# The test for over 128 tokens moved behind the first stores, and the last sums and the last store cut in halves

## The reference, cut to what matters

```python
def moe_swiglu(h, w_router, w_gate, w_up, w_down):
    ...
    for e in range(N_EXPERTS):
        ye = swiglu(t, w_gate[e], w_up[e], w_down[e]).astype(jnp.float32)
        out = out + gates[:, e:e + 1] * ye
...
        x = x + rms_norm(f_out, post_ffn_gain[l])
    return x
```

## Time and profile before

| | |
|---|---|
| median of 3 runs | 1172.28 us (1172.23 to 1173.7) |
| the profiled execution's own time | 1173.94 us |
| its span in the trace | 1172.2 us |
| PE busy | 1111.1 us (95%) |
| DVE busy | 889.5 us (76%) |
| ACT busy | 750.3 us (64%) |
| stores of the output | 2 of 512 KB |

### The profile page before, as it was taken

The page is one execution under the profiler, slowest core; times in us unless marked ns, Lnnn a source line. Parts: engine busy times, 40 slices in busy tenths (PEclk is TensorE's granted clock), DMA queues, the critical chain, the costliest instruction groups (busy, mean ns, idle before and its releaser), DMA issues.

```text
span 1172.2 us, 13852 instructions
## 1 busy us (share of the span) xinstructions
PE 1111.1 (95%) x5410; PEld 927.7 (79%) x5410; DVE 889.5 (76%) x743; ACT 750.3 (64%) x738; POOL 40.1 (3%) x76
## 2 busy tenths in 40 slices
PE   5998999997996699999999999999999999999995
PEld 5986888885994588888888888888888888888783
DVE  5666545456276489888888989888898988888895
ACT  5555433445365177777777777777767777777764
POOL 3000000000001000000000000000000000001100
PEclk9999999998998699999999999999999999999998
DMA  8647655551424499999999999999999999999981
GB/s 264 239 155 249 201 193 179 179 179 58 149 93 165 175 344 375 388 377 383 383 377 394 373 372 396 371 385 384 371 387 382 374 388 383 379 370 373 397 305 74
DMA packets 174594, 350.65 MB, mean 299 GB/s; under 512 B 9248, under 2 KB 58416, under 8 KB 174528
## 3 DMA queue, kind: packets, MB, share of 16 engines
q1 hardware_dynamic: 169792, 332.96, 78.0%
q0 software_dynamic: 4592, 16.30, 4.1%
q10 hardware_dynamic: 144, 0.52, 0.2%
HBM read 343.97 MB, written 5.77 MB: 298 GB/s over the span
## 4 chain that ended last, share of the span: by engine, by line
PE 88%; DVE 6%; ACT 3%; issue 2%; DMA 1%; DVEq 0%; SPq 0%; ACTq 0%
PE ps L1140 28%; PE ps L1141 27%; PE ps L1142 27%; PE ps L1417 2%; DVE lo_gu L1899 1%; PE ps L1147 1%; DMA raw_gu<-in_w_in 1%; PE ps L1460 1%; PE ps L1218 1%; DVE lo_d L1906 1%; DVE rows L1647 0%; DMA raw_d<-in_moe_w_down 0%; DVE xt_lo L1629 0%; PE ps L1199 0%; PE ps L1334 0%
## 5 line engine op out<-in xcount | busy, mean ns | idle before, releaser
L1899 DVE TENSOR_TENSOR lo_gu<-raw_gu,hi_gu 128x2048 fp32r<-128x2048 f32 x176 | 396.2, 2290 | 64.7 <-ACT hi_gu L992 64.7
L1140 PE MATMUL ps<-hi_gu,xt_hi 128*128 128x512 f32 (+1 forms) x1040 | 405.1, 390 | 9.1 <-DVE xt_lo L1629 4.3
L1142 PE MATMUL ps<-hi_gu,xt_lo 128*128 128x512 f32 (+1 forms) x1040 | 398.7, 383 | 0.0
L1141 PE MATMUL ps<-lo_gu,xt_hi 128*128 128x512 f32 (+1 forms) x1040 | 398.1, 383 | 0.0
L992 ACT CAST hi_gu<-raw_gu 128x2048 fp32r<-128x2048 f32 x176 | 327.9, 1910 | 11.2 <-PE ps L1142 8.1
L1002 ACT CAST hi_d<-raw_d 128x1024 fp32r<-128x1024 f32 x172 | 172.2, 1050 | 132.8 <-PE ps L1142 132.8
L1140 PEld LDWEIGHTS ps<-hi_gu,xt_hi 128*128 128x128 f32 x1040 | 198.3, 191 | 47.9 <-DVE xt_lo L1629 5.5
L1142 PEld LDWEIGHTS ps<-hi_gu,xt_lo 128*128 128x128 f32 x1040 | 198.2, 191 | 38.2
L1141 PEld LDWEIGHTS ps<-lo_gu,xt_hi 128*128 128x128 f32 x1040 | 198.4, 191 | 35.3
L1906 DVE TENSOR_TENSOR lo_d<-raw_d,hi_d 128x1024 fp32r<-128x1024 f32 x172 | 202.8, 1220 | 18.3 <-ACT hi_d L1002 17.6
L1140 PE MATMUL ps<-hi_d,ht_hi 128*128 128x512 f32 x424 | 167.9, 396 | 0.3 <-DVE ht_lo L1913 0.3
(11 more groups left out here) (241 smaller groups left out, 784.4 us busy)
## 6 DMA issues: line engine op xcount, KB each, us to landing
raw_gu<-in_moe_w_gate SPq DMA_DIRECT2D x176, 512.0 KB, 5.8
raw_gu<-in_moe_w_up SPq DMA_DIRECT2D x176, 512.0 KB, 7.2
raw_d<-in_moe_w_down SPq DMA_DIRECT2D x88, 1024.0 KB, 7.9
raw_gu<-in_dense_w_gate SPq DMA_DIRECT2D x22, 512.0 KB, 3.7
raw_gu<-in_dense_w_up SPq DMA_DIRECT2D x22, 512.0 KB, 4.7
raw_d<-in_dense_w_down SPq DMA_DIRECT2D x11, 1024.0 KB, 4.8
raw_gu<-in_w_in SPq DMA_DIRECT2D x16, 512.0 KB, 8.7
raw_gu<-in_w_out SPq DMA_DIRECT2D x16, 512.0 KB, 6.8
```

What stands on the lines that cost most here:

```text
L1140: pe.matmul(o, a_hi, b_hi, start=first, stop=False)
L1141: pe.matmul(o, a_hi, b_lo, start=False, stop=False)
L1142: return pe.matmul(o, a_lo, b_hi, start=False, stop=last)
L1899: dve.tensor_tensor(flat_piece(lo_gu, slot_at), flat_piece(raw_gu, slot_at), flat_piece(hi_gu, slot_at).bitcast(F32), ALU.subtract).then_i ...
```

## The change

- The test for a second round (read, test, jump) goes from ahead of the last sums to the very end of each of DVE, ACT and SP. PE's stays where it is.
- The last sums go by column halves: four of 128x512, in the order in which PE's four scatters end, each with its own semaphore step, where before there were two of 128x1024.
- The new `finish` does the gain, the reciprocal and the residual sum of one tile; tile 0 is finished ahead of tile 1's gain multiply. The result goes to `acc`, no longer to `x_res`. Tile 1's residual sum is cut into two column halves.
- SP stores tile 0 and the left half of tile 1; the right half is stored by ACT's queue.
- If there is a second round, it starts from `rows`, takes a norm of its own (two more columns in `sum_sq`, `root`, `rstd`) and stores both tiles once more. It doesn't run with these inputs.

```diff
@@ SP
+            sp.wait_ge(x_updated, FINAL + 1)
+            sp.dma_start(out[0, 0:P, :], acc[:, 0, :]).then_inc(out_stored, 16)
+            sp.wait_ge(x_updated, FINAL + 2)
+            sp.dma_start(out[0, P:2 * P, 0:512], acc[:, 1, 0:512]).then_inc(out_stored, 16)
             sp.wait_ge(slots_ready, 1)
             count = sp.value_load(overflow[0:1, 0:1], min_val=0, max_val=S)
             with sp.If(count > P):
...
-            for t in range(TT):
-                sp.wait_ge(x_updated, TT * (2 * DEPTH - 1) + t + 1)
-                sp.dma_start(out[0, t * P:(t + 1) * P, :], x_res[:, t, :]).then_inc(out_stored, 16)
-            sp.wait_ge(out_stored, 16 * TT)
+            sp.wait_ge(out_stored, 16 * (TT + 1))
@@ ACT
             experts()
+            for t in range(TT):
+                act.wait_ge(summed, TT + t + 1)
+                norm(norm_id(1, POST_FFN, t), rows[:, t, :], y_sb[:], D)
+            act.wait_ge(x_updated, FINAL + TT + 1)
+            act.dma_start(out[0, P:2 * P, 512:D], acc[:, 1, 512:D]).then_inc(out_stored, 16)
             act.wait_ge(slots_ready, 1)
             count = act.value_load(overflow[0:1, 0:1], min_val=0, max_val=S)
             with act.If(count > P):
                 overflow_experts()
-            for t in range(TT):
-                act.wait_ge(summed, t + 1)
-                norm(norm_id(1, POST_FFN, t), rows[:, t, :], y_sb[:], D)
@@ PE
-                        last = pe.matmul(o, picks, half_of(xt_lo, 0)[:, ks, :], start=False, stop=True)
-                        if n == 1:
-                            last.then_inc(last_scattered, 1)
+                        pe.matmul(o, picks, half_of(xt_lo, 0)[:, ks, :], start=False, stop=True
+                                  ).then_inc(last_scattered, 1)
@@ DVE
+            def finish(idx, total, to, pieces):
+
+                s, fill = gain_of(1, POST_FFN)
+                t = idx % TT
+                dve.wait_ge(gain_loaded[s], gain_level(s, fill))
+                dve.tensor_tensor(to[:, t, :], total[:, t, :], gains[s][:], ALU.mult).then_inc(gained, 1)
+                r = scale_of(idx)
+                dve.wait_ge(gained, idx - norm_id(1, POST_FFN, 0) + 1)
+                for n in range(pieces):
+                    cols = slice(n * D // pieces, (n + 1) * D // pieces)
+                    dve.scalar_tensor_tensor(to[:, t, cols], to[:, t, cols], r, x_res[:, t, cols], ALU.mult, ALU.add
+                                             ).then_inc(x_updated, 1)
...
             experts()
+            for n in range(2):
+                cols = slice(n * 512, (n + 1) * 512)
+                for t in range(TT):
+                    dve.wait_ge(last_scattered, n * TT + t + 1)
+                    dve.scalar_tensor_tensor(rows[:, t, cols], ps[:, B_GU + 2 * t + n, :], last_gate[:, t:t + 1],
+                                             acc[:, t, cols], ALU.mult, ALU.add).then_inc(summed, 1)
+            dve.wait_ge(summed, 2 * TT)
+            for t in range(TT):
+                finish(norm_id(1, POST_FFN, t), rows, acc, t + 1)
             count = dve.value_load(overflow[0:1, 0:1], min_val=0, max_val=S)
             with dve.If(count > P):
                 overflow_experts()
-            s, fill = gain_of(1, POST_FFN)
-            dve.wait_ge(gain_loaded[s], gain_level(s, fill))
-            for t in range(TT):
-                add_last(t, rows).then_inc(summed, 1)
-                dve.wait_ge(summed, t + 1)
-                dve.tensor_tensor(acc[:, t, :], rows[:, t, :], gains[s][:], ALU.mult).then_inc(gained, 1)
-            for t in range(TT):
-                r = scale_of(norm_id(1, POST_FFN, t))
-                dve.wait_ge(gained, t + 1)
-                dve.scalar_tensor_tensor(x_res[:, t, :], acc[:, t, :], r, x_res[:, t, :], ALU.mult, ALU.add
-                                         ).then_inc(x_updated, 1)
```

More of the change, by code:

```diff
@@ L166, in build_trunk @@
         eps = sb("eps", [P, 1])
-        sum_sq = sb("sum_sq", [P, 12 * TT])
-        root = sb("root", [P, 12 * TT])
-        rstd = sb("rstd", [P, 12 * TT])
+        sum_sq = sb("sum_sq", [P, 13 * TT])
+        root = sb("root", [P, 13 * TT])
+        rstd = sb("rstd", [P, 13 * TT])
         sinks = sb("sinks", [P, DEPTH, N_HEADS])
@@ L397, in build_trunk @@
         out_stored = sem("out_stored")
+        FINAL = TT * (2 * DEPTH - 1)
         gain_plan = []
@@ L604, in _ @@
             with sp.If(count > P):
-                sp.wait_ge(early_summed, TT)
+                sp.wait_ge(last_added, TT)
                 for t in range(TT):
@@ L613, in _ @@
                         load_expert(i, q, e, None)
-            for t in range(TT):
-                sp.wait_ge(x_updated, TT * (2 * DEPTH - 1) + t + 1)
-                sp.dma_start(out[0, t * P:(t + 1) * P, :], x_res[:, t, :]).then_inc(out_stored, 16)
-            sp.wait_ge(out_stored, 16 * TT)
+                for t in range(TT):
+                    sp.wait_ge(x_updated, FINAL + TT + 1 + t + 1)
+                    sp.dma_start(out[0, t * P:(t + 1) * P, :], rows[:, t, :]).then_inc(out_stored, 16)
+                sp.wait_ge(out_stored, 16 * (2 * TT + 1))
+            sp.wait_ge(out_stored, 16 * (TT + 1))
         @block.gpsimd
@@ L1096, in overflow_experts @@
             def overflow_experts():
+                act.wait_ge(last_lo_done, 2)
+                act.copy(spare[:, 2:3], eps[:, 0:1]).then_inc(y_copied, 1)
                 with act.Fori(0, E // 2) as i:
@@ L1114, in overflow_experts @@
                         act.copy(y_sb[:], banks(B_Y, 2)).then_inc(y_copied, 1)
+                act.wait_ge(expert_added, TT * E)
+                for t in range(TT):
+                    norm(6 * DEPTH * TT + t, acc[:, t, :], y_sb[:], D)
             act.wait_ge(const_made, 4)
@@ L1990, in experts @@
                 dve.wait_ge(last_gate_ready, 1)
[L1992 to L1995, removed]
+            def finish(idx, total, to, pieces):
[9 more added lines that the diff above has]
+                                             ).then_inc(x_updated, 1)
             def overflow_experts():
+                dve.wait_ge(out_stored, 16 * (TT + 1))
                 for t in range(TT):
-                    add_last(t, acc).then_inc(last_added, 1)
+                    dve.tensor_copy(acc[:, t, :], rows[:, t, :]).then_inc(last_added, 1)
                 dve.wait_ge(last_added, TT)
-                dve.memset(last_gate[:], 0.0).then_inc(last_gate_ready, 1)
                 with dve.Fori(0, E // 2) as i:
@@ L2025, in overflow_experts @@
                 dve.wait_ge(expert_added, TT * E)
-                dve.wait_ge(last_gate_ready, 2)
+                for t in range(TT):
+                    finish(6 * DEPTH * TT + t, acc, rows, 1)
             dve.wait_ge(const_made, 4)
```

## The result

The changed kernel takes 1177.27 us, median of 22 runs (1174.85 to 1178.09); the kernel before, run beside it, takes 1175.11 us, median of 22 (1170.68 to 1176.63). The ratio is 1.0022, with a 95% interval of 1.0015 to 1.003: slower by 0.22%, 2.2 to 2.6 us. I had forecast 1170.2 us, 2.1 us faster, in a range of 1168.9 to 1172.1. The direction was wrong, and so was the range.

What follows compares the result with a forecast made beforehand. TensorE bounds the whole span, but VectorE's late sums bound the end; VectorE gains 3.06 us, about 1 us is given back to ScalarE's final jump, so 1172.28 − 2.1 = 1170.2 us, range 1168.9 to 1172.1.

Steps and rivals of the forecast that it cites:

- none of that is touched: Everything before the last 15 us, TensorE's chain with its weight loads: claimed unaffected, so no cost was counted there.
- a second fetch at the end: Rival at the final jumps: instructions up to the barrier need two fetches; time 1174.8 us, chance 0.06.
- rival 1: At the end, ScalarE's jump is hidden and the stores end the span; time 1168.9 us, chance 0.13.
- rival 2: At the end, ScalarE's instruction fetch slips by 1.9 us behind data packets; time 1171.0 to 1172.1 us, chance 0.17.
- The jump leaves the head: VectorE behind the last xt_lo: the first half sum starts at 1157.98 instead of 1161.34, 3.36 us earlier.
- Half sums: VectorE's last sums: four halves, 0.67 us from start to start, the last ending at 1160.74.
- Two finishes: VectorE's gain, reciprocal and residual steps for both tiles: ends at 1166.06 instead of 1169.12, 3.06 us earlier.
- ScalarE: Squares and roots at the end: both 1.28 us table loads go, roots ready before the reciprocals, price nothing.
- The jumps arrive at the end: Final jumps: ScalarE's branch ends at 1167.3, its 2.5 us jump finishes last at 1169.8, span ends 1170.1.
- The stores: Last output stores: a half lands in 2.0 to 2.7 us, by 1168.1 to 1168.8, before ScalarE's jump is through.
- From span to time: Conversion to kernel time: the span's 2.1 us gain was taken whole off the unprofiled median.
- The base: Starting time of the forecast: median 1172.28 us without a profile, from three runs spanning 1.5 us.

Runs made afterwards that it cites:

- x6: x5 with SyncE reading and jumping early and issuing all stores, ScalarE storing nothing, VectorE reading early; ratio to the kernel before 1.0033, end 11.70 us.
- x7: x5 with SyncE issuing all three stores, then reading and jumping, and ScalarE issuing none; ratio to the kernel before 1.0036, end 12.80 us.
- x1: Changed kernel with 32 unused bytes per partition more behind the norm tensors; ratio to the kernel before 1.0034, stage 759.9 us.
- x5: Changed kernel with 96 unused bytes per partition more behind the norm tensors; ratio to the kernel before 1.0042, end 12.70 us.
- x8: x5 with the count read ahead of the stores or VectorE's last weight halves, branches left in place; ratio to the kernel before 1.0038, end 12.62 us.
- x9: Changed kernel with every later buffer at the old kernel's addresses under a 64-byte pad; 1167.15 us, ratio to the kernel before 0.9944.
- x12: Kernel before with hi_d, lo_d, xt_hi and all behind them shifted by 64 bytes; ratio to the kernel before 1.0119, stage 766.8 us.

## Why the prediction was wrong

**The step that failed is in its first paragraph: "none of that is touched".** It is true of the instructions and false of the addresses. Tensors that grew by 8 bytes pushed two operands of TensorE, the engine that bounds the kernel, to another place. The sum has this term at nothing; it measured 4.3 us (3.5 in the experts, 0.8 in the dense network), and that outweighs the 2.0 us won. The trace of before gave a hint at most: its down projection steps by 229, 232, 226 ns, and gate and up by an even 227. But the two more columns stood in the diff, and that tensors behind them move, and that TensorE's 88% of the chain read from them, could have been asked. My only case on the slow side, a second fetch at the end (0.06), was another mechanism; it did not occur. Nor did the two others: ScalarE's jump was not hidden (rival 1), and an instruction packet ran at 1172.4, 0.9 us behind its branch and not 2.8 (rival 2).

**The end was right**, by its steps. *The jump leaves the head:* first half sum 0.61 us behind `xt_lo`'s start, forecast 0.61. *Half sums:* 0.66 us from start to start, forecast 0.67. *Two finishes:* VectorE's end 8.63 us behind `xt_lo`, forecast 8.69. *ScalarE:* no table load behind 1153.3, roots never late. *The jumps arrive at the end:* ScalarE's branch ends at +9.91, forecast +9.93; its jump costs 2.6 us, forecast 2.5; it is the last engine; end at +12.81, forecast 12.73. x6 and x7 show that this jump is the limit. *The stores* were mis-sized: 2.9 us to landing for ScalarE's half where I took 2.0 to 2.7; it landed at 1173.2, about half a microsecond too early to decide the end.

**From span to time** a term was missing. What lies around the span is 1.74 us in before and 2.0 to 2.2 us in every execution of the kernels in which ScalarE's jump ends last (after, x1, x5, x8, x9), but 1.7 to 1.9 in every one of the others: 0.3 us more. So of the 2.0 us at the end 1.7 are left in the time. With it the sum of the profiled runs closes: stage +3.5, end −2.0, around the span +0.3, and +0.7 ahead of `last_gate`, together +2.5; own times 1176.46 − 1173.94 = 2.52.

The +0.7 ahead of `last_gate` has three parts: +2.2 us before the dense network's first down matmul, +0.8 in its down projection, which is the addresses' work, and −2.2 from its end to `last_gate` (120.35 us before, 118.11 after). The last of these goes with TensorE's clock. The window behind the dense network, first of before, then of after (the third number from the right is the granted clock):

```profile
280.00:320.00 40.00, 32.72 (x233) 31.54 (x232) 18.37 (x17) 16.35 (x27) 1.60 (x3) 0.83 0.36 126
```

```profile
280.00:320.00 40.00, 32.27 (x236) 30.65 (x237) 18.50 (x18) 18.59 (x29) 1.61 (x3) 0.91 0.37 128
```

These are means of 2.4 and 1.2 GHz: TensorE runs at the lower level for a longer part of it in before. In the 14 traces this part takes 117.4 to 118.2 us where the window shows 0.91 (seven of them), and 119.7 to 120.4 where it shows 0.83 to 0.87 (the other seven), whatever the kernel.

**The base** was low as well. The three runs shown ahead (1172.28) lie at the low side of 22 (median 1175.11). So 1170.2 would have been 2.8 us too low even with the right sign. Of the 6 us by which the time varies from run to run, some 2 go with this clock behind the dense network. It agrees that of 20 more executions of before five of the six with a mean clock of 0.978 took 1170.6 to 1171.3 us, and all 14 with 0.975 to 0.977 took 1172.2 to 1176.6. What makes up the rest stays open.

**Still open:** why TensorE steps slower at a distance that isn't a multiple of 256 bytes. That remainders matter is shown at six values. That it is the distance, and not the places of both operands, rests on x12 alone, where the down projection falls into the steps of before with both operands moved. In all runs with a distance of 0 both operands have the remainder 128; no run has that distance at another remainder, which would be the plainest test.

## What to carry to other kernels

A change that resizes any tensor changes the addresses of all behind it: list the operand addresses of the bounding engine before and after, and compare with a kernel that has the old code and the new addresses, which here told a 2.0 us gain from a 4.3 us loss. This change was good at its own place, and needed other addresses to show it. A jump over code costs 2.5 to 3.6 us wherever nothing hides it: moved behind the last store it still costs 1.0 us here (x6), and a jump that is taken ahead of the last stores costs nothing that shows.

## What the runs showed of the hardware

With operands of the type fp32r (the high and low parts), 128x128 stationary and 512 columns moving, at a granted clock of 1.00, matmuls step by 227 ns if stationary and moving operand lie a multiple of 256 bytes apart, and by medians of 226 to 235 ns at five other remainders. The experts' stage takes 752.3 us at best and 766.8 at worst with the same matmuls, and the old code 0.9965 to 1.0119 of its time before by its addresses alone. The Trainium skill ("SBUF — State Buffer", Operand start alignment) lets an operand start at any multiple of its element size. All the places here are of that kind, and nothing contradicts it; but it tells what is allowed, not what it costs, and the runs show that places differ in pace. The first seven steps of the neighbouring projection are uneven too (up to 236 ns in x5) though its own operands did not move.

Jumps over the second round took 2.6 us (ScalarE), 3.15 (VectorE), 2.85 (SyncE) and 3.5 (TensorE) in the changed kernel, and 3.2 on ScalarE in x8: the cost of one place does not carry over to another to better than half a microsecond.
